# Decode attention over a paged cache: the page gathers wait for half of a scoring pass as well

## The reference, cut to what matters

```python
def one_seq(args):
    pt, ql, qr, cn, kn = args
    ckv = jnp.concatenate([cache_ckv[layer, pt].reshape(past, KV_LORA), cn], axis=0)
    kr = jnp.concatenate([cache_kr[layer, pt].reshape(past, ROPE_DIM), kn], axis=0)
    return _latent_attention(ql[None], qr[None], ckv[None], kr[None], q_pos, k_pos)[0]

def _latent_attention(q_lat, q_rope, ckv, kr, q_pos, k_pos):
    scores = (jnp.einsum("bqhc,btc->bhqt", q_lat, ckv)
              + jnp.einsum("bqhr,btr->bhqt", q_rope, kr)).astype(jnp.float32) * MLA_SCALE
    scores = jnp.where(k_pos[None, :] <= q_pos[:, None], scores, NEG_INF)
    p = jax.nn.softmax(scores, axis=-1).astype(ckv.dtype)
    return jnp.einsum("bhqt,btc->bqhc", p, ckv)
```

## Time and profile before

| what | value |
| --- | --- |
| median of 3 executions | 1487.53 us (1483.99 to 1487.86) |
| the profiled execution, own time | 1485.23 us |
| the profiled execution, span | 1483.4 us |
| PE busy in the span | 1417.8 us (96%) |
| decode steps 12 to 52 (11 steps with gathers beside them) | 459.77 to 662.26 us |
| decode steps 56 and 60 | 662.26 to 682.46 us |
| POOL: page gathers, rotary gathers by indirect DMA | 64 and 32 |

### The profile page before, as it was taken

One profiled execution on the slowest core, in us unless ns is written; L12 is line 12 of the kernel. 1 busy time (PEld: TensorE's weight loads), 2 busy tenths in 40 slices (PEclk: granted clock), 3 DMA queues, 4 the chain that ended last, 5 costly groups with the idle time before them and its releaser, 6 DMA issues.

```text
span 1483.4 us, 28032 instructions
## 1 busy us (share of the span) xinstructions
PE 1417.8 (96%) x11192; PEld 1229.7 (83%) x11192; DVE 834.6 (56%) x1615; ACT 516.1 (35%) x1102; POOL 245.0 (17%) x193
## 2 busy tenths in 40 slices
PE   7999999999988988899899999999999999999997
PEld 7998977777655555556699999999999999999885
DVE  3484367667665444444567577664444445467745
ACT  3322466665432222223533334433333334113100
POOL 3110057664533333320100000000000000000000
PEclk9999999999998777789899999999999999999999
DMA  6552020001644434537621212123333337451722
GB/s 246 173 172 72 1 86 1 1 1 65 201 157 129 133 127 133 180 127 287 244 57 44 88 44 81 51 65 96 118 103 95 97 118 253 152 210 67 264 92 71
DMA packets 108437, 174.37 MB, mean 118 GB/s; under 512 B 14002, under 2 KB 77298, under 8 KB 107028
## 3 DMA queue, kind: packets, MB, share of 16 engines
q1 hardware_dynamic: 98068, 136.92, 28.0%
q0 software_dynamic: 10240, 35.66, 7.1%
HBM read 138.49 MB, written 34.06 MB: 116 GB/s over the span
## 4 chain that ended last, share of the span: by engine, by line
PE 50%; DVE 0%; issue 0%; ACT 0%; DVEq 0%
PE ps L2460 34%; PE ps L2491 10%; PE ps L2525 6%; PE ps L2511 0%; DVE p_h L2833 0%; DVE p_h L2836 0%; DVE p_stats L2820 0%; DVE p_h L2816 0%; PE ps L2501 0%; DVE p_mv L2827 0%; ACT p_rt L2608 0%; DVE p_rs L2831 0%; DVE p_stats L2825 0%; DVE p_stats L2824 0%; DVE p_ve L2829 0%
## 5 line engine op out<-in xcount | busy, mean ns | idle before, releaser
L2460 PE MATMUL ps<-p_x,p_w 128*128 128x272 f32 x4032 | 508.7, 289 | 1.0 <-PEq L1991 0.7
L2460 PEld LDWEIGHTS ps<-p_x,p_w 128*128 128x128 f32 x4032 | 508.3, 189 | 1.5 <-issue 1.5
L1535 PE MATMUL ps<-p_kT,p_q_rows 32*64 32x256 f32 x2048 | 129.7, 509 | 29.8 <-issue 23.9
L2491 PE MATMUL ps<-p_uh,p_w 128*128 128x352 f32 (+1 forms) x576 | 141.9, 327 | 0.0
L1535 PEld LDWEIGHTS ps<-p_kT,p_q_rows 32*64 32x64 f32 x2048 | 74.0, 174 | 76.7 <-issue 68.2
L987 POOL TENSOR_SCALAR p_pr<-p_pr,p_rec 128x896 f32<-128x896 f32 (+3 forms) x64 | 109.8, 1725 | 140.5 <-DVE p_rec L951 140.3
L2710 DVE TENSOR_TENSOR p_w<-p_sum,p_w 128x512 fp32r<-128x512 f32 x94 | 65.0, 691 | 119.1 <-ACT p_w L1918 119.0
L1918 ACT ACTIVATE p_w<-p_wr 128x512 fp32r<-128x512 f32 x96 | 60.2, 627 | 131.4 <-PE ps L2491 76.0
L2491 PEld LDWEIGHTS ps<-p_uh,p_w 128*128 128x128 f32 x576 | 101.8, 188 | 0.0
L1703 DVE CUSTOM_DVE_ANT_0 p_sc<-ps,p_zero 128x256 f32<-128x256 f32 x64 | 23.3, 421 | 139.4 <-PE ps L1542 88.5
L2491 PE MATMUL ps<-p_ul,p_w 128*128 128x352 f32 (+1 forms) x288 | 94.3, 328 | 0.0
(11 more groups left out here) (338 smaller groups left out, 2489.2 us busy)
## 6 DMA issues: line engine op xcount, KB each, us to landing
p_wr<-w_in SPq DMA_DIRECT2D x48, 512.0 KB, 3.6
g_kept<-p_slots SPq DMA_DIRECT2D x48, 272.0 KB, 2.5
p_ring<-g_kept SPq DMA_DIRECT2D x16, 544.0 KB, 5.0
p_x<-x_kept SPq DMA_DIRECT2D x6, 1088.0 KB, 7.2
t_kept<-p_t_raw SPq DMA_DIRECT2D x16, 272.0 KB, 2.4
p_x<-t_kept SPq DMA_DIRECT2D x4, 1088.0 KB, 9.1
p_gy<-g_kept SPq DMA_DIRECT2D x8, 544.0 KB, 5.7
p_xs<-x_prompt SPq DMA_DIRECT2D x8, 512.0 KB, 4.2
```

The lines of the kernel that those rows point to most:

```text
L1535: pe.matmul(cols(i, f), q_rows[rows, b % 2, d, :], kT[rows, x:x + S, 2 * f:2 * f + 2, d, :], start=(d == 0), stop=False, tile_position=(32 ...
L2460: last = pe.matmul(ps[:, lo + z, 0:PW], w[:, q % NW, part, t, :], v[:, t, z * PW:(z + 1) * PW], start=(i in STARTS and t == 0 and n == 0), ...
L2491: last = pe.matmul(ps[:, BANK_OF[g % 8], 0:tn], w[:, q % NW, part, t, :], v[:, t0:t0 + tn], start=(t == 0 and z == 0), stop=(t == KH - 1 a ...
```

## The change

A new semaphore, `half_scored`, is raised once in every step, on the last matmul of the first half (d = 3 of 0 to 7) of the L1535 products. Each page gather now waits for it too: those of the loop's round n until the first half of step n + 4 is done (its count is then n / 4 + 2). No instruction changes its place on any engine, and no other wait is changed.

```diff
+        half_scored = sem("half_scored")
...
                     for f in range(2):
                         for i in range(4):
                             rows = slice(32 * i, 32 * (i + 1))
-                            pe.matmul(cols(i, f), q_rows[rows, b % 2, d, :], kT[rows, x:x + S, 2 * f:2 * f + 2, d, :],
-                                      start=(d == 0), stop=False, tile_position=(32 * i, f * R))
+                            last = pe.matmul(cols(i, f), q_rows[rows, b % 2, d, :],
+                                             kT[rows, x:x + S, 2 * f:2 * f + 2, d, :], start=(d == 0), stop=False,
+                                             tile_position=(32 * i, f * R))
+                    if d == NB // 2 - 1:
+                        last.then_inc(half_scored, 1)
...
                 for x in range(n + NAT - LAG, n + NAT - LAG + S):
                     if NAT <= x < NG:
                         pool.wait_ge(pv_done, x - NAT + 1)
+                        pool.wait_ge(half_scored, n // S + 2)
                         gather_pages(nc, a, e, x)
```

## The result

| what | before | after |
| --- | --- | --- |
| median of 6 executions each | 1484.32 us (1479.14 to 1487.86) | 1474.23 us (1472.06 to 1476.81) |
| the profiled execution, own time | 1485.23 us | 1473.2 us |
| the profiled execution, span | 1483.4 us | 1471.3 us |

The ratio is 0.9938, with a 95% interval of 0.9922 to 0.9954. The change makes the kernel faster by 0.6%, some 10 us, where 37 were predicted.

The account below looks back on a forecast made before the run. Eleven decode steps beside gathers were taken to lose 92.5 us, TensorE trickling in a window on its scoring. Six short steps at 12.7 and five long at 17.8 sum to 165.2 against 202.5, 37.3 less: 1450 us, range 1400 to 1490.

Parts of the forecast that it names:

- The 92.5 us of excess: Eleven decode steps (12 to 52) beside gathers take 202.49 us against 110.0 undisturbed; all that placing gathers can win.
- A wait on an engine that already idles: nothing: The new increment and wait on POOL, which already idles 10 to 12 us there, were to cost nothing.
- T + 0: T is the end of a step's first half of L1535 scoring products, where the gathers were to start.
- The window opens 3.0 to 3.4 us after the first issue and closes 1.0 us after the last one's end, whatever PE does then: TensorE's slow stretch beside a run of gathers; with the change placed at T + 3.2 to T + 8.9.
- Long steps, 17.8 us: Window catches the second half's last 15 scoring passes; 16.1 us plus 1.7 for the clock.
- Short steps, 12.7 us: Scoring ends at T + 2.2, ahead of the window; value products meet it; 11.9 us plus 0.8 for the clock.
- The rate of 3.0 passes per us on value products: PE's pace inside the window, taken from the part ahead of decode: 17 passes in 5.7 us.
- The copies at T + 8.9 at worst, covered: In short steps DVE's copies of the scores were to finish before the next step's start at T + 10.1.
- B: Rival: trickle as hard on value products as on scoring, half the clock cost; short 14.8, long 18.7 us; 1475, chance 0.18.
- A: Rival: value work is not touched, the window hurts only dense work; 89 us less, 1398, chance 0.17.
- C: Rival: no change; gathers do not slow PE, or B with the whole clock cost; 1486, chance 0.12.
- D: Rival: window opens by passes since the first issue, about 54, so it closes on scoring again; 1507, chance 0.15.

Follow-up runs that it names:

- five: Kernel before, but a decode page gather waits until the one two groups ahead has landed, not four: 1417.59 us, ratio 0.9555.
- ten: Kernel before, with all rotary parts copied by SyncE's queue and none gathered by GpSimd: 1423.08 us, ratio 0.9617.
- eleven: Kernel before, with all rotary parts copied by SyncE's queue and page gathers awaiting the landing two groups back, not four: 1406.73 us, ratio 0.9519.
- experiment three: The change, with the semaphore raised behind the first quarter of a step's scoring products (32 of 128 passes), not the half: 1497.57 us, ratio 1.0107.
- two: The change with the new wait in short steps only; long steps issue gathers as before: 1470.15 us, ratio 0.99 to the kernel before.
- twelve: Kernel before, with pages and rotary parts all copied by SyncE's queue and no gathers issued by GpSimd: 1547.53 us, ratio 1.0477.
- thin gathers: Kernel before, with decode page gathers bringing 512 bytes a partition instead of 4 KB, same number of DMAs: 1484.44 us, ratio 0.9998.
- experiment one: The change, but in long steps page gathers wait for the whole scoring instead of its first half: 1456.16 us, ratio 0.9811 to the kernel before.

## Why the prediction was wrong

**The 92.5 us of excess, and that they belong to the gathers:** right. Experiments five, ten and eleven took 68, 55 and 74 us of the eleven steps' 202.5 away with the same work done, by changing nothing but how the gathers are issued.

**"A wait on an engine that already idles: nothing"; the gather within 0.1 us behind the 64th pass:** wrong by 1.2 us. GpSimd's first gather stands 3.0 to 3.1 us behind the step's start in all eleven steps, and 2.15 behind it in the quarter version. T + 0 in the prediction is T + 1.2. Of this 0.9 us is GpSimd's own way from the wait's end to the gather, and it stood in the trace of the kernel before: MOVE at 569.3, gather at 570.17. It costs nothing where a gather may start at any time, but here the place of the first gather is the change. In short steps this shifts the end of everything by 1.2 us. In long steps it puts the first issue just on the second half of the scoring.

**"The window opens 3.0 to 3.4 us after the first issue and closes 1.0 us after the last one's end, whatever PE does then":** the step that failed. The close held (1.05 to 1.3 us). The opening didn't: TensorE's first slow pass comes 1.3 us behind the first issue in a short step of the change, and about 1.6 in a long one. I had read the 3.0 to 3.4 from two steps in which sparse value work ran beside the first issues, and experiment three speaks for it that the opening depends on what PE does. Together with GpSimd's later start the window is T + 2.6 or T + 2.8 to T + 10.1, not T + 3.2 to T + 8.9.

**Long steps, 17.8 us:** measured 20.1 in step 24. I let the window catch the last 15 of 80 passes. It opens half a microsecond earlier, which is 19 dense passes: 18 of scoring and all 16 rotary ones were caught, and they ended at T + 10.5, not T + 8.9. The rest, 5.3 us without a fall of the clock, took 7.8, not 7.0 with the 1.7 I gave the clock. 1.6 + 0.8 us, less 0.1 ahead of T, make the 2.3 between 17.8 and 20.1. Over five steps, 89.0 predicted and 103.4 measured: **14.4 of the miss**.

**Short steps, 12.7 us:** measured 14.5 in three, 88.1 for all six instead of 76.2: **11.9 of the miss**. The 128 passes on L1535 (now L1536) were rightly placed ahead of the window. The 16 rotary passes behind them weren't: they take 2.27 us, and scoring ends at T + 4.0, not T + 2.2. The clock did better than my 0.8 us, none being lost in the three typical ones (the 16.1 and 15.7 us are steps 12 and 36, at clock 0.90 and 0.89). The rate of 3.0 passes per us on value products came near: 12 of the first 16 in the 4.6 us from 538.77 to 543.33, 2.6 per us. That is luck. The 3.0 was read at 390 to 395 us for a stretch "with gathers issued tightly", but the gathers there start at 389.82, 392.63 and 394.43, and of the 1.2 us that PE idles in it, 0.92 end with VectorE. And the rate didn't decide alone. ScalarE's copy, without which the other 16 can't start, waits for a signal of TensorE, and that came 1.3 us behind the run's end. So a short step is 3.0 us to the first gather, 7.6 for the run, 1.3 for the signal, 0.6 for ScalarE's copy and 1.9 for 16 value passes: 14.4. That wait isn't in the prediction at all. It is a floor just above what the trickle gives by itself: in step 28 the 20 value passes that are left at 543.33 would need 2.3 us at 117 ns, so by my estimate the step would have been some 0.4 us shorter without the wait. Only in step 12, where the first 16 passes were through by 470.1, does TensorE stand idle for it, 3.04 us. A quicker trickle in the others would have met the same floor. "The copies at T + 8.9 at worst, covered" hangs on a signal of the same kind: they start at T + 10.1 and end 1.1 us before they are needed.

**The sum:** 165.2 predicted, 191.5 measured; 14.4 + 11.9 = 26.3 us, all of it in these two terms. Outside the eleven steps little moved. The rest of the span, behind step 60, is 2.1 us shorter, and step 12 starts 0.7 us later, which no part of the change explains; step 56 takes 11.5 us (group 63's gather, at most 0.5 predicted, 0.3 measured), step 60 8.99.

**The rivals.** B, the trickle as hard on value products, came nearest by its time, 1475 against 1474, with 14.8 us for a short step, but by a reason that isn't the one: PE passed more than B's 5 to 11, and waited for a signal. Its 18.7 for a long step was too low. A is out, since value products do stall. C is out by experiments two, five and ten. D, priced at 1507, isn't what the change does; a quarter comes near it, with 1498. It was to decide if scoring in a short step didn't end by T + 2.5, and scoring did end later, at T + 4.0; but no pass on L1536 was caught there. It warned of the right place, the dense work just behind the first issues, with the wrong rule. On traffic, the Trainium skill's page "SBUF — State Buffer", section "SBUF: two separate sides", is borne out: 215 GB/s with the clock at 1.00, and no difference from a third of the bytes. Where it lets a matmul wait for nobody, the runs here show otherwise: a run of GpSimd's indirect DMAs does hold TensorE up, by another way than bandwidth. The same page's box on DMAs from GpSimd's queue advises the queues of SyncE or ScalarE, for another case, a DMA that VectorE's work holds up; experiments ten and twelve show what that is worth here and where it ends, at SyncE's 0.6 us an issue.

**What stays open.** What inside the chip ties TensorE to GpSimd's issues isn't shown. The runs leave room for the way by which instructions reach TensorE, and for the way by which its semaphore increments leave it. That both are late in the same stretch speaks for something shared. A late load of TensorE's code is not it, at least in step 36 of the kernel before: the trace has no packet of an instruction queue between 570.5 and 579.8 us, and TensorE stalls and goes on again (578.83) within that time.

## What to carry to other kernels

When an engine stalls on "issue" beside another engine's work, find out first what of that work does it: bytes, number, or spacing. Two small edits (thin gathers, two in flight) told more than the whole placing of the run; and this placing gave 10 us, the best one tried 29 (experiment one), where breaking the run gave 67 to 73. Before a wait's place is counted on, read from the trace how long its engine takes from the wait's end to its next instruction. A limit on transfers in flight is also a pace for their issues: look at how tightly the issues follow each other, not only at how many transfers the queue can bear. And when work is moved into a disturbance, test the rates in the piece that it is moved onto; a rate from a sparser stretch isn't one.

## What the runs showed of the hardware that was not expected

- A run of indirect DMAs issued by GpSimd 1.32 us apart starves TensorE, sooner (1.3 us) where its work was dense already than where it was sparse (1.6 to 3.4 us). With the page gathers mostly 2 to 4 us apart it costs 2.2 us a step instead of 8.4, at 215 GB/s.
- In such a run, what TensorE signals comes late: the semaphores went up, and VectorE and ScalarE started, 5 us behind the matmuls, 1.05 to 1.3 us behind the run's end, while VectorE's wait for a landing in the same run ended in it (538.72).
- Fewer bytes for a gather can cost time: with two in flight, pages an eighth the size were 27 us slower, since they land sooner and let the issues close up.
- Behind a wait, GpSimd takes 0.9 us from the wait's end to the start of an indirect DMA (533.7 to 534.61 us with the change, 569.3 to 570.17 before).
- A page gather takes 5.1 to 5.4 us from issue to the next issue, if each waits for the one ahead to land; a DMA of SyncE's queue takes that queue about 0.6 us.
